# The input projection of a hybrid trunk as seven block products for eight

## The chip, the cores and the metric

One core of a Trainium2 chip (trn2). The metric is the device time of one execution in microseconds (us); lower is better.

## The reference

One layer over x (2,048 tokens by 1,024 channels, float32). The input projection takes RMS-normed x through one weight of 1,024 by 10,256 columns; its columns feed a state space mixer, a windowed attention, a short convolution, and three merge gates.

```python
h = rms_norm(x, norm_pre)
proj = h @ w_in
(z, xbc, dt_raw, q, k, v, g_attn, u, b_sc, c_sc, g_sc, merge) = split(proj)
y_ssm = ssd_branch(z, xbc, dt_raw, ...)              # xbc: silu(conv4(xbc) + b); z: silu
y_attn = attention_branch(q, k, v) * silu(g_attn)
y_sc = b_sc * conv3(c_sc * u) * silu(g_sc)
merged = sum(sigmoid(merge_i) * (y_i @ p_i))
out = x + rms_norm(merged @ w_out, norm_post)
```

## The kernel before

Five stages run one after another: the input projection (`projection_stage`, L88 to L596), the SSD scan with the second half of the gates (`ssd_gates_stage`), attention, the merging of the branches, the output. The change is in the first; the second only reads its operands in another layout.

Every float32 product is made of three matmuls on values split in a high part (rounded to `float32r`) and a low part (the rest): hi x hi, hi x lo, lo x hi. In the projection the weight tile (128 channels of the contraction by 128 columns) is the stationary operand, and 512 tokens of h move.

The opening (L299 to L310 on PE): x comes in 16 tiles of 128 tokens; DVE sums the squares (L486), ACT takes the root (L353) and scales (L359), POOL multiplies by `norm_pre` (L258), PE turns the tile (L279), ACT takes the high part (L363) and DVE the low one (L496). The turned h stays in two buffers, `h0` for the first half of the tokens and `h1` for the second. The dt product is interleaved with it.

Then 88 tiles of 128 columns follow in the loops from L311 on. `product` (L291) waits for its weights and its accumulator and makes 96 matmuls, 24 for each of four spans of 512 tokens; the 24 gate tiles make the first half of the tokens alone, 48 matmuls. Two slots alternate, each with four banks of PSUM, so a slot's tile is read while the other is made. The order is that of the columns: z, xbc, q, k and v, g, sc, gates.

```python
for c in chunks:
    h_hi, h_lo = (h[t // 2][:, t % 2 * 4:t % 2 * 4 + 4, part, c] for part in range(2))
    pe.matmul(to, w_hi[:, slot, c], h_hi, start=c == 0, stop=False)
    pe.matmul(to, w_hi[:, slot, c], h_lo, start=False, stop=False)
    last = pe.matmul(to, w_lo[:, slot, c], h_hi, start=False, stop=c == KC - 1)
```

SP loads each weight tile (512 KB, L166) once its slot's weights are made. POOL rounds it (L247) and subtracts (L249) when the slot's product has ended. ACT evacuates z, k, v, g and the gates (L393) and issues their stores; xbc is convolved by DVE out of PSUM (L523, L528), then ACT's silu; q is split by ACT (L423) and DVE (L540); sc is multiplied by DVE (L549 to L561). The chain that makes dt and its sums (L566 to L595) runs among the gates.

Of the kernel before, what the change touches and what calls it, by code (L numbers as in the profile page):

```python
# [10 lines left out]

# [5 lines left out]
F32 = mybir.dt.float32  # L17
# [4 lines left out]
P = 128  # L22
# [65 lines left out]
def projection_stage(nc, w, d, h, wt, v, ident, eps):  # L88
# [9 lines left out]
    pairs = {"z": SSM // P // 2, "xbc": (C_DT - C_XBC) // P // 2, "q0": KV // P // 2, "q1": KV // P // 2,  # L98
             "q2": KV // P // 2, "kv": 2 * KV // P // 2, "g": KV // P // 2,
             "sc": 4 * SC // P // 2, "gates": 3 * DM // P // 2}  # L100
    base, n_pairs = {}, 0
    for kind, n in pairs.items():
        base[kind] = n_pairs
        n_pairs += n
    with ExitStack() as stack:
        s = Scope(nc, stack)
        cleared, cleared_sems = s.cleared_sem, lambda name, n: [s.cleared_sem(f"{name}{i}") for i in range(n)]
        raw, w_hi, w_lo, work = wt["raw"], wt["w_hi"], wt["w_lo"], wt["work"]
        stage = s.sb("p_stage", [P, 2, SEQ])
# [4 lines left out]
        w_pre = s.sb("n_wpre", [P, DM])  # L114
        ssum, std, rstd = (s.sb(n, [P, 4]) for n in ("n_ssum", "n_std", "n_rstd"))
        acc = s.ps("p_acc", [P, 2, SEQ])

        x_sb = stage[:].rearrange("p a (b n) -> p (a b) n", n=DM)
        x_scaled, h_tok = (work[:, k].rearrange("p (b n) -> p b n", n=DM) for k in range(2))
        tr = acc[:, 1].rearrange("p (b n) -> p b n", n=DM)  # L120
        squared = raw[:, 1].rearrange("p c n -> p (c n)")

        dt_raw = work[:HEADS, 0]
        t0, t1, t2, t3 = (work[:, 1, j * TILES * HEADS:(j + 1) * TILES * HEADS] for j in range(4))
        ps_dt, ps_cs, ps_last = (acc[:, 1, at:at + TILES * HEADS] for at in (2 * BANK, 3 * BANK, 3 * BANK + TILES * HEADS))
# [1803 lines left out]
```

## Time and profile before

| | |
|---|---|
| time, median of 3 runs (lowest to highest) | 3249.74 us (3247.03 to 3251.0) |
| the profiled execution's own time | 3249.21 us |
| its span, first to last instruction | 3247.6 us |
| busy PE, PE weight load | 3074.1 us (95%), 2586.7 us (80%) |
| busy DVE, ACT, POOL | 1071.6, 861.0, 752.0 us (33, 27, 23%) |
| granted TensorE clock, mean | 0.979 |
| DMA, mean over the span | 119 GB/s |

The profile is of one execution. "Busy" of PE is counted from the start to the modelled end of each matmul, which overlap: a matmul of 512 columns is shown with about 0.39 us while the next starts 0.23 us after it. The pitch from start to start is what a matmul costs. A line such as L286 is a line of the kernel's source; PEld is the loading of stationary weights.

### The profile page before, as it was taken

The page shows a single profiled execution, that of the slowest core. Times are in us where ns is not written, and L with a number is a line of the kernel's source. Part 1 is how long each engine was busy: PE and PEld are TensorE (multiplying, and loading weights), DVE is VectorE, ACT ScalarE, POOL GpSimd, SP SyncE. Part 2 cuts the span into 40 slices and gives each one's busy share as a digit, 9 for nine tenths or more (in the row PEclk, how much of TensorE's full clock was granted, in tenths as well). Part 3 has the DMA queues.
Part 4 walks back from the last instruction along what each step waited for, and adds up shares of the span by engine and source line. Part 5 has one row for each costly group of instructions (what it writes and reads, how often), then busy time and mean ns, then how long its engine had stood idle before and what let it go on. Part 6 is the DMA issues. An engine that isn't in the chain of part 4 may idle for free. (4 is left out here: it accounts for less than half of the span.)

```text
span 3247.6 us, 41561 instructions
## 1 busy us (share of the span) xinstructions
PE 3074.1 (95%) x15182; PEld 2586.7 (80%) x15182; DVE 1071.6 (33%) x1824; ACT 861.0 (27%) x1461; POOL 752.0 (23%) x390
## 2 busy tenths in 40 slices
PE   6999999999999999999998999998999968989898
PEld 5888888888888888888887778777898856778687
DVE  6003444201000011110001544444565567762333
ACT  5110000000000000000112555554566542332232
POOL 7111111111111111112322443442111034321000
PEclk9999999999999999999999999998999989999999
DMA  5121121344412201112234564564534457775543
GB/s 156 58 77 65 71 77 68 93 117 129 116 59 77 77 20 38 39 39 86 97 97 132 148 174 136 155 174 171 157 119 144 144 176 237 235 244 145 174 136 116
DMA packets 335884, 387.70 MB, mean 119 GB/s; under 512 B 23104, under 2 KB 284480, under 8 KB 320192
## 3 DMA queue, kind: packets, MB, share of 16 engines
q1 hardware_dynamic: 317440, 287.42, 30.0%
q10 hardware_dynamic: 16080, 91.23, 8.1%
q0 software_dynamic: 2304, 8.39, 0.7%
q8 instruction: 21, 0.34, 0.0%
q14 instruction: 39, 0.32, 0.0%
HBM read 251.21 MB, written 135.79 MB: 119 GB/s over the span
## 5 line engine op out<-in xcount | busy, mean ns | idle before, releaser
L286 PE MATMUL p_acc<-h,w_hi 128*128 128x512 f32 x2464 | 970.0, 394 | 3.8 <-DVE h L496 3.5
L288 PE MATMUL p_acc<-h,w_lo 128*128 128x512 f32 x2464 | 966.0, 392 | 0.0
L287 PE MATMUL p_acc<-h,w_hi 128*128 128x512 f32 x2464 | 960.2, 390 | 0.0
L288 PEld LDWEIGHTS p_acc<-h,w_lo 128*128 128x128 f32 x2464 | 463.1, 188 | 103.9
L286 PEld LDWEIGHTS p_acc<-h,w_hi 128*128 128x128 f32 x2464 | 463.7, 188 | 100.5 <-DVE h L496 4.8
L287 PEld LDWEIGHTS p_acc<-h,w_hi 128*128 128x128 f32 x2464 | 463.3, 188 | 101.0
L247 POOL CAST w_hi<-raw 128x1024 fp32r<-128x1024 f32 x88 | 91.4, 1039 | 1350.9 <-PE p_acc L288 1344.9
L1598 PE MATMUL b_acc<-b_yhi,b_whi 128*128 128x512 f32 x512 | 205.7, 402 | 43.8 <-DVE b_ylo_ssd L1689 25.8
L249 POOL TENSOR_TENSOR w_lo<-raw,w_hi 128x1024 fp32r<-128x1024 f32 x88 | 212.1, 2410 | 7.1
L393 ACT ACTIVATE p_stage<-p_acc 128x1024 f32<-128x1024 f32 (+1 forms) x45 | 64.2, 1427 | 554.3 <-PE p_acc L288 554.2
L1600 PE MATMUL b_acc<-b_yhi,b_wlo 128*128 128x512 f32 x512 | 202.6, 396 | 0.0
L1245 ACT ACTIVATE a_probs<-a_scores,a_att 128x256 f32<-128x256 f32 (+1 forms) x384 | 155.7, 454 | 108.4 <-DVE a_att L1278 106.9
L1278 DVE CUSTOM_DVE_ANT_0 a_scores<-a_pss,a_band 128x256 f32<-128x256 f32 (+1 forms) x384 | 125.1, 364 | 142.7 <-PE a_pss L1183 116.7
L779 PE MATMUL s_acc<-h,w_hi 128*128 128x512 f32 x384 | 168.5, 439 | 0.0
L523 DVE TENSOR_SCALAR work<-p_acc,p_cw,p_cb 128x2048 f32<-128x2048 f32 x16 | 38.6, 2411 | 384.4 <-PE p_acc L288 384.4
L1215 PE MATMUL a_pso<-a_vt,a_probst 128*128 128x65 f32 x1200 | 156.2, 269 | 1.5 <-DVE a_att L1291 1.5
L1598 PEld LDWEIGHTS b_acc<-b_yhi,b_whi 128*128 128x128 f32 x512 | 98.4, 192 | 69.8 <-issue 36.5
L781 PE MATMUL s_acc<-h,w_lo 128*128 128x512 f32 x384 | 152.5, 397 | 0.0
L780 PE MATMUL s_acc<-h,w_hi 128*128 128x512 f32 x384 | 152.5, 397 | 0.0
L1215 PEld LDWEIGHTS a_pso<-a_vt,a_probst 128*128 128x128 f32 x1200 | 149.9, 193 | 2.0 <-DVE a_att L1291 1.8
L549 DVE TENSOR_TENSOR work<-p_acc,work 128x2048 f32<-128x2048 f32 x4 | 9.2, 2292 | 417.4 <-PE p_acc L288 417.4
L1183 PE MATMUL a_pss<-a_khi,a_q 128*128 128x256 f32 (+1 forms) x384 | 128.1, 356 | 19.6 <-DVE a_att L1278 19.1
(195 smaller groups left out, 4141.4 us busy)
## 6 DMA issues: line engine op xcount, KB each, us to landing
raw<-w_in SPq DMA_DIRECT2D x113, 512.0 KB, 4.4
a_q<-s_qs SPq DMA_DIRECT2D x27, 1024.0 KB, 4.9
b_gate<-s_gates SPq DMA_DIRECT2D x48, 512.0 KB, 7.1
s_xbc<-p_stage ACTq DMA_DIRECT2D x16, 1024.0 KB, 3.9
work<-s_xbc SPq DMA_DIRECT2D x16, 1024.0 KB, 7.1
s_sums<-s_cs SPq DMA_DIRECT2D x16, 1024.0 KB, 5.1
b_att<-s_att SPq DMA_DIRECT2D x24, 528.0 KB, 5.6
s_qs<-p_stage ACTq DMA_DIRECT2D x24, 512.0 KB, 5.5
```

The lines of the kernel that those rows point to most:

```text
L249: pool.tensor_tensor(w_lo[:, slot], raw[:, slot], w_hi[:, slot], ALU.subtract).then_inc(w_made[slot], 1)
L286: pe.matmul(to, w_hi[:, slot, c], h_hi, start=c == 0, stop=False)
L287: pe.matmul(to, w_hi[:, slot, c], h_lo, start=False, stop=False)
L288: last = pe.matmul(to, w_lo[:, slot, c], h_hi, start=False, stop=c == KC - 1)
L779: pe.matmul(acc_tiled, w_hi[:, slot, b], hi, start=b == 0, stop=False)
L780: pe.matmul(acc_tiled, w_hi[:, slot, b], lo, start=False, stop=False)
L781: last = pe.matmul(acc_tiled, w_lo[:, slot, b], hi, start=False, stop=b == KC - 1)
L1183: last = pe.matmul(bank[:, (e + 1) * 2 * P - n:(e + 1) * 2 * P], q_s[:, g, at:at + P], keys, start=first, stop=not first)
L1215: last = pe.matmul(ps_o[:, j // 2 % 2, (b + e) % 4, :OUT_W], probs_t[:, j % 4, 2 * e + h], v_tok[:, g, b + e - 1 + h, sl * OUT_W:(sl + 1) ...
L1245: last = act.activation(probs[:, j % 4, e, 2 * P - n:], scores[:, j % 4, e, 2 * P - n:], ACT.Exp, bias=att[:, g, b + e, 2 * OUT_W + sl:2 * ...
L1598: pe.matmul(to, w_hi[:, k, c], y_hi[:, c, span], start=c == at, stop=False)
L1600: last = pe.matmul(to, w_lo[:, k, c], y_hi[:, c, span], start=False, stop=c == at + n - 1)
```

## The change

The projection's weights of two tiles (256 columns) and 1,024 tokens are seen as 2 by 2 blocks on each side: A11, A12 are the two halves of the contraction of the first tile, A21, A22 those of the second; B11, B21 are the two halves of the contraction for 512 tokens, B12, B22 for the next 512. Instead of 8 block products of 12 matmuls, 7 are made (Winograd's form of Strassen's scheme), each of 12 matmuls over 4 chunks. A "set" is the seven products of one pair of tiles for one half of the tokens: 44 sets for the first half (gates, kv, g, q, xbc, sc, z) and 32 for the second, 76 in all, unrolled.

- Weight sums, POOL: four passes of 128x512 a set (`add_sums`), then seven subtractions for the low parts (`lo`). The high parts go to ACT (`split_weight`), each after the product of the set before that read the same buffer. `w_hi` and `w_lo` hold seven blocks, once.
- Products, PE: X, R0, R1, W, X, R0, W name the banks of the seven; four banks of PSUM serve them, each once. The other four are for the convolution.
- Output sums: ACT copies product 1 (`product_one`), DVE makes seven sums of 128x512 a set, into the stage or, for q, xbc and sc, into a padded buffer in SBUF, from which the convolution now reads; two small buffers carry the last tokens of the first half to the second.
- Activations: B11, B22 and so on and T1 to T4, their differences, are made once for each half, split into seven operands of 128x2048, which take the place of `h0` and `h1`. For the second half the blocks are prepared during sets 1 to 12 through DRAM (`s_h`, `s_t`), and the seven operands are loaded and split again at the turn, sets 43 and 44.
- dt is two products of 32 columns, 32 matmuls each, after sets 41 and 44, and its chain runs in sets 46 to 48. All stores are issued by SP, none by ACT.

The diff, cut to its core (setup of buffers, the order's tables, the dt chain and the preparation of B are left out):

```diff
-                def span_of(slot, t, chunks=range(KC)):
...
-                with pe.Fori(0, base["gates"]) as i:
-                    product(1, i)
-                    product(0, i + 1)
...
+                for u in range(NSETS):
+                    half = SETS[u][2]
+                    for k in range(PRODUCTS):
+                        bank = acc[:, bank_of[k]]
+                        if u in (0, TURN):
+                            pe.wait_ge(op_ready[k], half + 1)
+                        pe.wait_ge(w_made, PRODUCTS * u + k + 1)
+                        if k == 0 and u:
+                            pe.wait_ge(mixed_in, SUMS * u - 2)
+                        if k == 1 and u:
+                            pe.wait_ge(mixed_in, SUMS * u - 1)
+                        if k == 3 and u:
+                            pe.wait_ge(mixed_in, SUMS * u)
+                        if k == 4:
+                            pe.wait_ge(p1_made, u + 1)
+                        if k == 5:
+                            pe.wait_ge(mixed_in, SUMS * u + 1)
+                        if k == 6:
+                            pe.wait_ge(mixed_in, SUMS * u + 4)
+                        for c in range(4):
+                            hi, lo = (x[:, k, c * P:(c + 1) * P] for x in (w_hi, w_lo))
+                            pe.matmul(bank, hi, ops[k][:, 0, c], start=c == 0, stop=False)
+                            pe.matmul(bank, hi, ops[k][:, 1, c], start=False, stop=False)
+                            last = pe.matmul(bank, lo, ops[k][:, 0, c], start=False, stop=c == 3)
+                        last.then_inc(prod, 1)
...
-                def split(slot, use, n):
-                    pool.wait_ge(raw_loaded[slot], 16 * use + 16)
-                    wait_alone(pool, acc_made[slot], use + 1, carried)
-                    pool.tensor_copy(w_hi[:, slot], raw[:, slot]).then_inc(hi_ready, 1)
-                    pool.wait_ge(hi_ready, n + 1)
-                    pool.tensor_tensor(w_lo[:, slot], raw[:, slot], w_hi[:, slot], ALU.subtract
-                                       ).then_inc(w_made[slot], 1)
...
+                def lo(u, k):
+                    if u:
+                        pool.wait_ge(hi_made, PRODUCTS * (u - 1) + k + 1)
+                    tt(w_lo[:, k], weight(u, k), w_hi[:, k], ALU.subtract).then_inc(w_made, 1)
+
+                def add_sums(u):
+                    a11, a12, a21, a22 = (raw[u % 2 * 2 + m][:, 4 * k:4 * k + 4].rearrange("p c n -> p (c n)")
+                                          for m in range(2) for k in range(2))
+                    tt(sums[:, 0], a21, a22, ALU.add).then_inc(sums_made, 1)
+                    pool.wait_ge(sums_made, 4 * u + 1)
+                    tt(sums[:, 1], sums[:, 0], a11, ALU.subtract).then_inc(sums_made, 1)
+                    tt(sums[:, 2], a21, a11, ALU.subtract).then_inc(sums_made, 1)
+                    pool.wait_ge(sums_made, 4 * u + 2)
+                    tt(sums[:, 3], a12, sums[:, 1], ALU.subtract).then_inc(sums_made, 1)
...
+                def product_one(u):
+                    act.wait_ge(prod, PRODUCTS * u + 1)
+                    if u:
+                        act.wait_ge(mixed_in, SUMS * u - 2)
+                    act.activation(p1 if u else p1_first, acc[:, X], ACT.Copy).then_inc(p1_made, 1)
+
+                def split_weight(u, k):
+                    act.wait_ge(prod, PRODUCTS * (u - 1) + k + 1)
...
+                    act.activation(w_hi[:, k], weight(u, k), ACT.Copy).then_inc(hi_made, 1)
...
+                    if u:
+                        finish(u - 1)
...
+                    tt(t_now, acc[:, R0], p1 if u else p1_first, ALU.add).then_inc(mixed_in, 1)
...
+                    tt(u_now, acc[:, R1], t_now, ALU.add).then_inc(mixed_in, 1)
...
+                    tt(out_block(u, 1, 1), acc[:, W], u_now, ALU.add).then_inc(mixed_in, 1)
+                    tt(t_now, acc[:, W], t_now, ALU.add).then_inc(mixed_in, 1)
...
+                    tt(out_block(u, 0, 0), acc[:, X], p1 if u else p1_first, ALU.add).then_inc(mixed_in, 1)
+                    dve.wait_ge(prod, PRODUCTS * u + 6)
+                    tt(out_block(u, 0, 1), acc[:, R0], u_now, ALU.add).then_inc(mixed_in, 1)
...
+                    tt(out_block(u, 1, 0), acc[:, W], t_now, ALU.add).then_inc(mixed_in, 1)
```

How the order moves, at three places. On POOL, before, one pass of the loop over two weight tiles (`raw` are the loaded tiles):

```order
L247 CAST w_hi<-raw 128x1024 [waits p_acc_made1]
L248 ISA
L249 TENSOR_TENSOR w_lo<-raw,w_hi 128x1024 [waits p_hi_ready]
L245 ISA
L84 REGISTER_ALU [waits p_raw_loaded0]
L247 CAST w_hi<-raw 128x1024 [waits p_acc_made0]
```

and now, one set (`p_sums` are the four weight sums, `p_hi_r` ACT's high parts):

```order
L398 TENSOR_TENSOR p_sums<-raw 128x512 [waits p_hi_r,p_w_made,p_raw_loaded1,p_raw_loaded0]
L400 TENSOR_TENSOR p_sums<-p_sums,raw 128x512 [waits p_sums_r]
L401 TENSOR_TENSOR p_sums<-raw 128x512
L403 TENSOR_TENSOR p_sums<-raw,p_sums 128x512 [waits p_sums_r]
L393 TENSOR_TENSOR w_lo<-raw,w_hi 128x512 [waits p_hi_r]
L393 TENSOR_TENSOR w_lo<-p_sums,w_hi 128x512 [waits p_hi_r] x3
L393 TENSOR_TENSOR w_lo<-raw,w_hi 128x512 [waits p_hi_r]
```

With the two that follow, eleven passes of 512 stand where two casts and two subtractions of 1,024 stood for as many columns, and they are made once for each half of the tokens.

On DVE, before, the convolution of one xbc tile:

```order
L523 TENSOR_SCALAR work<-p_acc,p_cw,p_cb 128x2048
L527 ISA
L528 ISA [waits p_conv_step]
L528 SCALAR_TENSOR_TENSOR work<-p_acc,p_cw,work 128x2045
L527 REGISTER_ALU
L528 ISA [waits p_conv_step]
L528 SCALAR_TENSOR_TENSOR work<-p_acc,p_cw,work 128x2046
```

and now, from the sixth sum of a set to the first sums of the next (`p_halo` carries tokens between the halves, `p_sums_r2` counts the sums, `p_prod` the products):

```order
L875 TENSOR_TENSOR work<-p_acc,work 128x512 [waits p_prod]
L709 COPY work<-p_halo 128x3 [waits p_posted]
L713 COPY p_halo<-work 128x3 [waits p_sums_r2,p_step]
L714 TENSOR_SCALAR p_acc<-work,p_cw,p_cb 128x1024
L718 SCALAR_TENSOR_TENSOR p_acc<-work,p_cw,p_acc 128x1024 [waits p_step]
L887 TENSOR_TENSOR work<-p_acc,work 128x512 [waits p_sums_r2,p_prod]
L718 SCALAR_TENSOR_TENSOR p_acc<-work,p_cw,p_acc 128x1024 [waits p_step] x2
L709 COPY work<-p_halo 128x3 [waits p_posted]
L713 COPY p_halo<-work 128x3 [waits p_sums_r2,p_step]
L714 TENSOR_SCALAR p_acc<-work,p_cw,p_cb 128x1024
L718 SCALAR_TENSOR_TENSOR p_acc<-work,p_cw,p_acc 128x1024 [waits p_step] x3
L811 TENSOR_TENSOR work<-p_acc,work 128x512 [waits p_sums_r2,p_p1_r,p_prod]
```

The sums that release PSUM banks now stand between the passes of the convolution.

On PE, the step from one product to the next, before (once in 96 or 48 matmuls) and now (once in 12):

```order
L293 REGISTER_ALU [waits p_w_made1]
L286 MATMUL p_acc<-h0,w_hi 128x512 [waits p_acc_taken1]
L287 MATMUL p_acc<-h0,w_hi 128x512
L288 MATMUL p_acc<-h0,w_lo 128x512
```

```order
L489 MATMUL p_acc<-h_kept,w_lo 128x512
L487 MATMUL p_acc<-p_ops,w_hi 128x512 [waits p_sums_r2,p_w_made]
L488 MATMUL p_acc<-p_ops,w_hi 128x512
```

`h_kept` and `p_ops` hold the operands of the seven products. 6,384 matmuls of L487 to L489 and 64 of the dt products stand where 7,392 of L286 to L288 were executed.

## Rows read from the trace of the kernel before

**Rows 1.** The page's busy time by engine.
```profile
PE 3074.1 (95%) x15182; PEld 2586.7 (80%) x15182; DVE 1071.6 (33%) x1824; ACT 861.0 (27%) x1461; POOL 752.0 (23%) x390
```

**Rows 2.** Groups by line (busy, mean ns, idle before, releaser), and L288's own answer.
```profile
L286 PE MATMUL p_acc<-h,w_hi 128*128 128x512 f32 x2464 | 970.0, 394 | 3.8 <-DVE h L496 3.5
L247 POOL CAST w_hi<-raw 128x1024 fp32r<-128x1024 f32 x88 | 91.4, 1039 | 1350.9 <-PE p_acc L288 1344.9
L249 POOL TENSOR_TENSOR w_lo<-raw,w_hi 128x1024 fp32r<-128x1024 f32 x88 | 212.1, 2410 | 7.1
...
L288 PE MATMUL p_acc<-h,w_lo x2464: 388/392/629, 30.6 to 1741.4; 128*128 128x512 f32 x190
```

**Rows 3.** Stretches of time: length, busy us of PE, PEld, DVE, ACT, POOL, PEclk, DMA share, GB/s.
```profile
1000.00:1200.00 200.00, 200.00 (x877) 164.44 (x876) 11.47 (x5) 13.21 (x7) 31.02 (x18) 1.00 0.18 56
1740.00:1750.00 10.00, 4.05 (x19) 3.38 (x18) 1.23 (x1) 3.61 (x4) 1.03 (x2) 0.84 0.36 115
```

**Rows 4.** PE in order of time, projection (start us, us).
```profile
71.74 0.50 PE L286 MATMUL p_acc<-h,w_hi 128*128 128x512 f32 x1 [0.26 <-POOL w_lo L249]
72.08 0.39 PE L287 MATMUL p_acc<-h,w_hi 128*128 128x512 f32 x1
...
1339.62 0.39 PE L288 MATMUL p_acc<-h,w_lo 128*128 128x512 f32 x1
...
1343.92 0.40 PE L286 MATMUL p_acc<-h,w_hi 128*128 128x512 f32 x1
```

**Rows 5.** PE in order of time, output stage; 13 matmuls stand between the two.
```profile
3149.65 0.39 PE L1833 MATMUL o_acc<-o_wlo,o_mhi 128*128 128x512 f32 x1
...
3152.82 0.39 PE L1832 MATMUL o_acc<-o_whi,o_mhi 128*128 128x512 f32 x1
```

**Rows 6.** Lines of POOL (ns, min/median/max) and of DVE (groups), several stages.
```profile
L1474 POOL TENSOR_TENSOR b_wlo<-b_raw,b_whi x20: 1266/4616/4959, 2638.4 to 3005.2; 128x2048 fp32r<-128x2048 f32 x12, 128x1536 fp32r<-128x1536 f32 x4, 128x512 fp32r<-128x512 f32 x4
...
L1486 POOL TENSOR_TENSOR b_att<-b_att x8: 1619/1630/2147, 2665.9 to 2851.5; 128x512 f32<-128x512 f32 x8
...
L258 POOL TENSOR_TENSOR work<-work,n_wpre x16: 2338/3314/3410, 9.4 to 59.7; 128x1024 f32<-128x1024 f32 x16
...
L909 DVE TENSOR_TENSOR s_cbm<-s_psm,v_tri 128x512 f32<-128x512 f32 x16 | 11.1, 692 | 76.7 <-PE s_psm L805 69.4 <-DMA s_norm<-ssm_norm 7.3
...
L1689 DVE TENSOR_TENSOR b_ylo<-b_ylo,b_yhi 128x1024 fp32r<-128x1024 f32 x12 | 20.3, 1750 | 6.1 <-ACT b_yhi L1508 6.1
```

**Rows 7.** POOL, then DVE, each in order of time, around two sc tiles.
```profile
1366.19 1.04 POOL L247 CAST w_hi<-raw 128x1024 fp32r<-128x1024 f32 x1 [18.40 <-PE p_acc L288]
1367.31 2.41 POOL L249 TENSOR_TENSOR w_lo<-raw,w_hi 128x1024 fp32r<-128x1024 f32 x1
...
1389.24 2.41 POOL L249 TENSOR_TENSOR w_lo<-raw,w_hi 128x1024 fp32r<-128x1024 f32 x1
...
1366.13 2.29 DVE L558 TENSOR_TENSOR work<-p_acc,work 128x2048 f32<-128x2048 f32 x1 [12.28 <-PE p_acc L288]
...
1390.00 3.80 DVE L561 TENSOR_TENSOR p_stage<-p_stage,work 128x2048 f32<-128x2048 f32 x1 [21.58 <-ACT p_stage L448]
```

**Rows 8.** Groups by line and shape, projection.
```profile
L528 DVE SCALAR_TENSOR_TENSOR work<-p_acc,p_cw,work 128x2047 f32<-128x2047 f32 x16 | 37.6, 2350 | 2.4 <-DVE work L528 2.3
...
L393 ACT ACTIVATE p_stage<-p_acc 128x1024 f32<-128x1024 f32 x24 | 24.6, 1025 | 231.4 <-PE p_acc L288 231.4
```

**Rows 9.** All engines in order of time, the opening.
```profile
6.27 1.23 DVE L486 CUSTOM_DVE_ANT_0 raw<-p_stage 128x1024 f32<-128x1024 f32 x1 [0.22 <-DMA p_stage<-x]
...
11.80 1.94 PE L279 MATMUL p_acc<-ident,work 128*128 128x128 f32 x8 [11.80 <-POOL work L258]
...
35.06 1.03 PE L279 MATMUL p_acc<-ident,work 128*128 128x128 f32 x8
```

**Rows 10.** DMA issues: KB each, median us from issue to landing.
```profile
a_q<-s_qs SPq DMA_DIRECT2D x27, 1024.0 KB, 4.9
...
work<-s_xbc SPq DMA_DIRECT2D x16, 1024.0 KB, 7.1
```

More of the change, by code:

```diff
@@ new lines, in weight, with wait_stage, out_block @@
+        def weight(u, k):
+            which = weight_of[k]
+            if which[0] == "s":
+                return sums[:, which[1]]
+            return raw[u % 2 * 2 + which[1]][:, which[2] * 4:which[2] * 4 + 4].rearrange("p c n -> p (c n)")
+        def wait_stage(eng, u, slot):
+            n = stores_before(u, slot)
+            if n:
+                eng.wait_ge(stored[slot], 16 * n)
+        def out_block(u, m, n):
+            at = slice(n * BANK, (n + 1) * BANK)
+            return body[m][:, at] if padded(SETS[u][0]) else stage[:, u % 2 * 2 + m, at]
@@ new lines, in _ @@
+                        last = pe.transpose(acc[:, c, j * P:(j + 1) * P], x_tile(j)[:, c * P:(c + 1) * P], ident[:])
+                last.then_inc(turned, 1)
+                pe.wait_ge(scaled, 8)
+                for c in range(KC):
+                    pe.wait_ge(ev_dve if c % 2 else ev_act, c // 2 + 1)
+                    for j in range(4):
+                        last = pe.transpose(acc[:, c, j * P:(j + 1) * P], x_tile(4 + j)[:, c * P:(c + 1) * P], ident[:])
+                last.then_inc(turned, 1)
@@ new lines, in _, with dt_product @@
+                pe.wait_ge(ev_act, 8)
+                pe.wait_ge(ev_dve, 8)
+                def dt_product(half):
+                    pe.wait_ge(dtw_made, 4)
+                    for n, terms in enumerate((((0, 0), (4, 4)), ((8, 5), (0, 3)))):
+                        for first, k in terms:
+                            for c in range(4):
+                                for part in range(2):
+                                    last = pe.matmul(acc[:2 * HEADS, CV + n], dt_w[:, first + c], ops[k][:, part, c],
+                                                     start=(first, k, c, part) == (*terms[0], 0, 0),
+                                                     stop=(first, k, c, part) == (*terms[1], 3, 1))
+                    last.then_inc(dt_prod, 1)
@@ L771, in gates @@
                             j, part = 3 * k + half // 2, half % 2
-                            slot, first = (j // 2 + 2) % 3, 4 * (j % 2)
+                            slot = (j // 2 + 2) % 3
                             if part == 0:
```

1058 lines of the change are left out of this document (626 added, 432 removed).

## Prediction

> **What bounds the kernel now.** I read the page's table of busy time first: PE is busy for 95% of the span, every other engine for a third or less [rows 1]. The groups by line then show where: the input projection's three matmuls (L286 to L288), 2,464 each, 7,392 in all [rows 2]. The stretches of time show them alone on the path: PE is busy for 200.00 of 200 us at a granted clock of 1.00 and falls to 4.05 of 10 where the stage ends [rows 3]. Inside it the others wait for PE, not the reverse: POOL's L247 sat idle 1,344.9 us before L288 released it [rows 2]. So a matmul less is its whole pitch saved, as long as the others keep up with the rest. After the opening the 7,296 matmuls from 71.74 us (the first of the weight tile after the dt product [rows 4]) to 1741.4 [rows 2] take 1,669.7 / 7,295 = 0.2289 us each; the end of a product runs at 0.2263 (19 steps from 1339.62 to 1343.92 [rows 4]), and the output stage, with a whole 512-wide operand and a wait every six matmuls, at 3.17 / 14 = 0.2264 [rows 5].
>
> **What goes and what comes on PE.** 7,392 matmuls go. 76 sets of 7 products of 12 matmuls come, 6,384, and 64 for dt: 944 fewer, each still 512 wide. For the pitch of the new ones the two bounds are 0.2264 [rows 5] and 0.2289; I take 0.2278, between them, since the order of waits is like the output stage's but a product alternates between operand buffers. A set is then 84 x 0.2278 = 19.1 us, a product 2.73 us.
>
> **POOL's share of a set.** 11 passes of 128x512, where the tile before had a cast and a subtraction of 128x1024. A subtraction takes 2,410 ns for 1,024 [rows 2] and at best 1,266 for 512 [rows 6]; with the 0.08 us between the cast (1366.19 + 1.04) and its follower (1367.31) [rows 7] that is 11 x 1.35 = 14.8 of 19.1 us. The set's last w_lo waits for the last product of the set before, but its reader is six products (16 us) away; the next four sums and six subtractions fit in between. I cost it at nothing; the cover is 4.3 us a set, and once it is gone every microsecond is one on PE, 75 times.
>
> **DVE's share.** Seven passes of 512 with one operand in PSUM, 0.69 each (L909 [rows 6]): 4.8 us. In the 16 xbc sets come two tiles of one scaled copy and three taps at 1,024: by halves of the 2,350 for 2,047 [rows 8], about 1.2 each, 9.8 us, and about 2 us of halo copies and hand-overs: 16.6 of 19.1. By position: the last sum ends 1.6 us into the next set (R0's sum, the copy and one or two taps of the first tile lie ahead of it), the remaining taps reach to about 10 us, T's sum is made at 10.7 and product 5 asks for it at 13.6. It fits with 3 us to spare, at nothing. Shorter kinds have more room. **ACT** has seven halves of a 1,025 ns copy [rows 8], P1's copy and two 1,024-wide passes: about 0.59 x 8 + 2.1 = 6.8 us, hidden.
>
> Here a contention shows: L561, both operands in SBUF, took 3.80 us from 1390.00, while POOL subtracted from 1389.24 to 1391.65; L558, 2,048 as well but with one operand in PSUM, took 2.29 from 1366.13, beside POOL's cast and 1.1 us of its subtraction [rows 7]. POOL's 2,410 did not grow. The sums of this change read PSUM, so I take them as L558; the q tiles' subtraction, the gated products of sc and the operand splits do not.
> The Trainium skill (SBUF — State Buffer, section "Who interferes with whom") says that a DVE instruction with two SBUF inputs and a GpSimd one that reads SBUF exclude each other for a whole instruction, so POOL would also be held: by that rule a q set gives POOL 14.8 + 2.4 us, still under 19.1, and the sum stays within its range. The trace agrees on DVE's side (1391.65 + 2.29 = 1393.94 against 1393.80 measured); POOL being held shows in L258's 3,314 ns against 2,338 at best [rows 6].
>
> **The opening.** Before, the first product starts near 30 and the first weight tile after dt at 71.74 [rows 2, 4]. Now nothing of set 0 can start before all eight x tiles of the first half are scaled and turned. The second tile is read at 6.27 [rows 9]; with two weight loads between, at 1.5 to 2 us for each 512 KB, the eighth lands near 22. ACT's square and root and DVE's scale put it at 27; 32 transposes at the cold pace (1.94 for 8) end near 34, the evacuations near 37. Then product 0 starts, and the next operands follow one another: the differences T1 to T4 on DVE (2.3 each, up to 3.8 beside POOL), each split by ACT (1.9) and DVE (2.3). Passing down that chain: T1 39, T2 42, operand 1 ready 46, operand 2 49, operand 3 55, operand 6 62, the sums after it 64, and product 6 ends about 67; with the slow first matmuls set 1 starts at **69**. From both sides: 60 with every pass at its lone time, 85 if each of the nine DVE passes waits for POOL (9 x 1.5 more).
>
> **What else is put on PE.** B's transposes: eight groups of eight, 1.03 each warm [rows 9], 8.2 us. Those of dt and cs and two small matmuls, as before, about 3. The dt products 64 x 0.2278 = 14.6. **At the turn** between the halves seven operands of 1 MB are loaded as the products release them (4.9 us from issue to landing [rows 10]) and split by ACT (1.9) and DVE (seven passes of 2.3, or 3.8 beside POOL) among the running sums: DVE has 16 to 27 us more work within two sets and 13 us of room. By position operand 0 is ready at 16 of 19, operands 3 to 6 each a microsecond or two late: 6 us, between 0 and 20. The dt chain (L783 to L805) holds PE about 1 us. The B preparation through DRAM in sets 0 to 12 waits on SP for loads and stores of 1 MB or less (4.9 and 7.1 us [rows 10]) with a set of 19.1 us per step: at nothing; behind those waits on SP stand the weight loads, issued a set ahead, and the stores, whose slot is asked for 9 us into the second next set.
>
> **Sum.** End of the last product: 69 + 75 x 84 x 0.2278 (1,435.1) + 14.6 + 8.2 + 3 + 6 + 1 = 1,536.9, against 1,741.6 now: -204.7. The tail (POOL's last subtraction, silu of two tiles, a store) is 1.5 us longer than the 7 to 9 us now. The next stages keep their work. -203 from the profiled execution's 3,249.21 is **3,046 us**; that execution stands 0.5 below the median of the runs, which changes nothing.
>
> **Rivals.** (1) *Each product pays a hand-over.* 532 products start with a wait; where PE did wait, the first matmul's step was 0.34 instead of 0.23 (71.74 to 72.08 [rows 4]). 532 x 0.11 = +58: 3,104. For it: four banks, each read by DVE before reuse. Against: by position all are free 2 us or more ahead, and [rows 5] shows none. (2) *DVE is late in the xbc sets*: at the 1,750 ns that the dearest 1,024-wide pass takes (L1689 [rows 6]), eight passes are +4.2, 20.8 in all, 1.7 x 16 = +27: 3,073. (3) *POOL paces mildly*: at L1486's 1,695 ns [rows 6] the eleven are 19.5 us with gaps: 0.4 x 75 = +30: 3,076. (4) *POOL paces and the kernel is slower*: the saving is 203 / 75 = 2.7 us a set, gone once a set lasts 21.8 us, i.e. a POOL pass of 1.91 us. L1486's dearest is 2.147: 11 x 2.23 = 24.5, +405: 3,451. For it: POOL shares with DVE, and DVE is now busy in every set. Against: [rows 7] shows POOL at its pace, 2.41, beside L561. (5) *The change does not remove work*: excluded by the order of instructions for PE, unless the opening or the turn gives it back, which their upper bounds (16 and 14) don't.
> Unrolled code is a lesser one: PE has 7,742 rows for 2,059. The Trainium skill (Runtime: NRT & Kernel Launch, section "Instruction fetch mechanics") says straight code is fetched ahead and mostly hidden, taken branches not; no row here has so long a straight piece, so it neither adds nor takes.
>
> **How the numbers follow.** The forecast 0.71, (1) 0.08, (2) 0.07, (3) 0.07, (4) 0.03, other delays below the saving 0.04. The low end takes the pitch of 0.2264 (-9), the opening at 60 (-9) and no loss at the turn (-6): 3,022. The high end adds to the forecast the opening's 16, the turn's 14 and the pitch's 8, and takes in (2) and (3): 3,085. That leaves out (1), (4) and some of the rest, 0.15 to 0.2. A measurement of this kernel tells 0.2% (6.5 us) from no change: faster 0.96, same 0.01, slower 0.03.
>
> **What would show it.** Right: 6,384 matmuls at a pitch near 0.228 and PE at 100% from about 70 us on; the stage's last product ending near 1,537; POOL's 512-wide subtraction at 1.2 to 1.3 us; gaps on PE only before 70 us and around the middle. Wrong: PE idle in every set with POOL's w_lo as releaser (3, 4), in xbc sets with DVE (2), or a step of 0.34 at each product's first matmul (1).

## The result and the profile after

| | before | after |
|---|---|---|
| median | 3250.37 us | 3060.57 us (3056.77 to 3064.43) |
| ratio | | 0.9419, 95% interval 0.9398 to 0.9441 |
| profiled execution | 3249.21 us | 3064.23 us (span 3062.6) |
| last matmul of the projection starts at | 1741.4 us | 1553.4 us |

One of the four executions of the kernel before took 4392.04 us and is left out of the ratio; without it the median is 3249.74.

The kernel is 5.8% faster. The forecast was 3,046, the range 3,022 to 3,085: the time lies inside the range and 14.6 us above the forecast.

The page of after, busy time by engine, which answers to [rows 1]:

```profile
PE 2874.0 (94%) x14238; PEld 2412.6 (79%) x14238; DVE 1587.1 (52%) x2540; ACT 1211.7 (40%) x2094; POOL 1569.2 (51%) x1044
```

PE has 944 records less (15,182 to 14,238), exactly the difference that the prediction counts, and is busy 200 us less; POOL has doubled (752 to 1,569), DVE went from 1,072 to 1,587. The share of PE in the span is the same as before, 94 against 95%: the kernel is bound as it was, by less work.

The page's groups of after, and the answer for line L489, which answer to [rows 2] (busy us, mean ns | idle before, releaser; then ns min/median/max, first and last start):

```profile
L487 PE MATMUL p_acc<-h_kept,w_hi 128*128 128x512 f32 x1216 | 482.2, 397 | 14.3 <-DVE h_kept L673 7.8
L393 POOL TENSOR_TENSOR w_lo<-p_sums,w_hi 128x512 fp32r<-128x512 f32 x304 | 406.6, 1354 | 153.5 <-ACT w_hi L571 153.2
...
L571 ACT ACTIVATE w_hi<-p_sums 128x512 fp32r<-128x512 f32 x300 | 189.5, 632 | 492.1 <-PE p_acc L489 472.2
...
L489 PE MATMUL p_acc<-h_kept,w_lo x1216: 388/389/632, 34.1 to 1550.6; 128*128 128x512 f32 x174
L489 PE MATMUL p_acc<-p_ops,w_lo x912: 388/392/628, 43.7 to 1553.4; 128*128 128x512 f32 x183
```

Read the idle column: ACT's copies sat idle 472.2 us until PE's L489 released them, and POOL's subtraction waited for ACT 153.2 us. The order of who waits for whom is PE, then ACT, then POOL (before, POOL made the high parts itself and waited for PE directly); the weight chain is behind PE in time, not ahead of it. This pass of POOL is 1,354 ns on average, where the prediction took 1.35 with its gap.

Stretches of time of after, which answer to [rows 3] (length, busy us of PE, PEld, DVE, ACT, POOL, PEclk, DMA share, GB/s):

```profile
0.00:40.00 40.00, 17.98 (x76) 15.88 (x76) 22.15 (x27) 23.36 (x37) 27.15 (x26) 0.79 0.50 157
40.00:70.00 30.00, 19.54 (x67) 15.46 (x68) 23.77 (x12) 11.68 (x12) 28.46 (x16) 0.77 0.19 53
540.00:690.00 150.00, 150.00 (x656) 122.81 (x655) 141.44 (x147) 51.87 (x78) 110.67 (x87) 1.00 0.35 109
1300.00:1500.00 200.00, 200.00 (x875) 163.74 (x874) 90.69 (x100) 55.34 (x88) 152.77 (x115) 1.00 0.27 77
1550.00:1560.00 10.00, 3.76 (x17) 2.75 (x15) 3.68 (x3) 4.75 (x4) 2.41 (x1) 0.91 0.27 105
```

In steady sets PE is at 200.00 of 200 at a granted clock of 1.00. The convolutions of the xbc sets (540 to 690) are the densest stretch for DVE, 141.44 of 150, and PE loses nothing there. POOL is at 152.77 of 200 from 1,300 on, or 14.7 us a set against 14.8 predicted. The opening (40 to 70) is different: PE 19.54 of 30, POOL 28.46 of 30. The last row holds the stage's end, where PE falls to 3.76 of 10.

All of PE's waits of after from 40 to 1,560 us (us in total, times, longest):

```profile
PE p_acc L487 <- DVE h_kept L673: 7.8, 1, 7.8
PE p_acc L510 <- DVE v_all L801: 4.5, 1, 4.5
PE p_acc L487 <- DVE p_ops L673: 4.2, 1, 4.2
PE p_acc L487 <- DVE p_stage L873: 3.7, 1, 3.7
PE p_acc L487 <- DVE work L832: 0.4, 1, 0.4
```

Five waits, 20.6 us, all of them with DVE as releaser and none in a steady set: two in set 0 (7.8, 4.2), one at the turn (3.7), one in the dt chain (4.5), and 0.4 in set 3, beside the preparation of B. None has POOL's `w_lo`.

The same terms as in the prediction's sum, by the starts of the sets in the trace of after:

| term | predicted | measured | difference |
|---|---|---|---|
| set 1 starts | 69 | 71.3 | +2.3 |
| 75 sets of 84 matmuls | 1,435.1 (19.13 each) | 1,444.0 (19.25 each) | +8.9 |
| dt products (behind sets 41 and 44) | 14.6 | 14.8 | +0.2 |
| transposes of B (sets 1 to 8, with the wait of 0.4) | 8.2 | 7.8 | -0.4 |
| transposes of dt and cs (the 3 predicted held the two small matmuls too) | 3 | 1.7 | -1.3 |
| the turn (sets 43, 44) | 6 | 5.8 | -0.2 |
| dt chain with the two small matmuls (set 47: 27.38 instead of 19.25) | 1 | 8.1 | +7.1 |
| end of the last product | 1,536.9 | 1,553.6 | +16.7 |
| the rest of the span, longer than before by | 1.5 | 3 | +1.5 |

That is the profiled execution, 18 us above the forecast; its run lies 3.7 above the median. Three terms carry the miss: the pitch, the dt chain and the opening. The experiments below go at these, and before that at the ground under the forecast: that PE's work sets the time.

### The profile page after: what moved, and what is told of

It reads as the page before. It is cut to its first block and busy times, and to the rows that moved or that the text cites. A ratio compares the mean times of both kernels' runs of the same rounds, so it can differ in the third digit from the quotient of the medians.

```text
span 3062.6 us, 41517 instructions
## 1 busy us (share of the span) xinstructions
PE 2874.0 (94%) x14238; PEld 2412.6 (79%) x14238; DVE 1587.1 (52%) x2540; ACT 1211.7 (40%) x2094; POOL 1569.2 (51%) x1044
## 5 line engine op out<-in xcount | busy, mean ns | idle before, releaser
L487 PE MATMUL p_acc<-h_kept,w_hi 128*128 128x512 f32 x1216 | 482.2, 397 | 14.3 <-DVE h_kept L673 7.8
L393 POOL TENSOR_TENSOR w_lo<-p_sums,w_hi 128x512 fp32r<-128x512 f32 x304 | 406.6, 1354 | 153.5 <-ACT w_hi L571 153.2
L489 PE MATMUL p_acc<-h_kept,w_lo 128*128 128x512 f32 x1216 | 478.7, 394 | 0.0
L488 PE MATMUL p_acc<-h_kept,w_hi 128*128 128x512 f32 x1216 | 476.6, 392 | 0.0
L571 ACT ACTIVATE w_hi<-p_sums 128x512 fp32r<-128x512 f32 x300 | 189.5, 632 | 492.1 <-PE p_acc L489 472.2
L487 PE MATMUL p_acc<-p_ops,w_hi 128*128 128x512 f32 x912 | 360.9, 396 | 4.6 <-DVE p_ops L673 4.2
L489 PE MATMUL p_acc<-p_ops,w_lo 128*128 128x512 f32 x912 | 358.3, 393 | 0.0
L488 PE MATMUL p_acc<-p_ops,w_hi 128*128 128x512 f32 x912 | 355.9, 390 | 0.0
L487 PEld LDWEIGHTS p_acc<-h_kept,w_hi 128*128 128x128 f32 x1216 | 230.2, 189 | 63.7 <-DVE h_kept L673 8.2
L489 PEld LDWEIGHTS p_acc<-h_kept,w_lo 128*128 128x128 f32 x1216 | 230.2, 189 | 52.3
L488 PEld LDWEIGHTS p_acc<-h_kept,w_hi 128*128 128x128 f32 x1216 | 230.4, 189 | 50.5
L487 PEld LDWEIGHTS p_acc<-p_ops,w_hi 128*128 128x128 f32 x912 | 171.8, 188 | 42.1 <-DVE p_ops L673 4.9
L489 PEld LDWEIGHTS p_acc<-p_ops,w_lo 128*128 128x128 f32 x912 | 171.5, 188 | 40.8
L488 PEld LDWEIGHTS p_acc<-p_ops,w_hi 128*128 128x128 f32 x912 | 171.6, 188 | 38.2
```

The lines of the kernel that those rows point to most:

```text
L393: tt(w_lo[:, k], weight(u, k), w_hi[:, k], ALU.subtract).then_inc(w_made, 1)
L487: pe.matmul(bank, hi, ops[k][:, 0, c], start=c == 0, stop=False)
L488: pe.matmul(bank, hi, ops[k][:, 1, c], start=False, stop=False)
L489: last = pe.matmul(bank, lo, ops[k][:, 0, c], start=False, stop=c == 3)
L571: act.activation(w_hi[:, k], weight(u, k), ACT.Copy).then_inc(hi_made, 1)
```

## The experiments

The kernel before ran beside every one of them; its medians were 3245.53 to 3249.65 us. Later stages vary by some 15 us from one execution to the next (the rest after the projection was 1,502 to 1,523 us in these traces, at unchanged code), so for a change inside the projection the start of its last matmul in the trace is the sharper measure. All but e1 to e3 keep the amount of work. e1, e2, e3, e5, e6 and e10 have two executions each. Products are counted from 0 here, as in the code; the expectations count them from 1.

**e1: an eighth product.** Product 4 is made twice a set, on PE alone.

```diff
-                        for c in range(4):
+                        for c in list(range(4)) * (2 if k == 4 else 1):
```

> Product 5 of every set is made twice, 12 matmuls more in each of 76 sets, so eight products a set as without the block scheme; the result stays the same. Theory (PE's count of matmuls is the whole price): 912 x 0.227 = +207 us, 3,268 us, and about 18 us over the kernel before, which is what the opening, the turn and the dt chain cost. Rival (the others set the pace of a set, so PE has room): well under +150 us.

Measured: 3273.71 us, ratio 1.0079 (1.0053 to 1.0105). A set lasts 21.97 us, 2.72 more than after's 19.25; the last matmul starts at 1754.0, 200.7 later than in after. The gain comes wholly from the product left out: with eight products and all the rest of the change in place the kernel is 0.8% slower than before.

**e2 and e3: more work on POOL.** From set 2 on the first weight sum is made two or five times more, each waited for.

```diff
+                    for j in range(5 if u > 1 else 0):      # e2: range(2 ...)
+                        tt(sums[:, 0], a21, a22, ALU.add).then_inc(padded_made, 1)
+                        pool.wait_ge(padded_made, 5 * (u - 2) + j + 1)
                     tt(sums[:, 0], a21, a22, ALU.add).then_inc(sums_made, 1)
```

> POOL makes the first weight sum three times from set 2 on, two passes of 1.3 us more a set. Theory (POOL has some 4 us a set to spare): no change, within 5 us of 3,061. Rival (POOL sets the pace already in part): +2.7 x 74 = up to +200 us.

> Five passes more a set: 15.1 + 6.8 = 21.9 us of POOL in a set that lasts 19.25. Theory: POOL becomes the bound, 2.6 x 74 = +195 us, 3,255 us, as slow as the kernel before, with PE waiting for w_lo in every set. Rival (POOL's work is not what PE would wait for): no change.

Measured: e2 3085.29 us, ratio 0.9499 (0.9468 to 0.9530); e3 3217.91, ratio 0.9907 (0.9888 to 0.9927). The stretch of steady sets in e2, and then in e3:

```profile
1300.00:1500.00 200.00, 200.00 (x875) 163.75 (x874) 99.86 (x108) 55.62 (x90) 180.19 (x136) 1.00 0.28 81
```

```profile
1300.00:1500.00 200.00, 189.01 (x801) 149.97 (x799) 153.90 (x146) 55.33 (x91) 195.37 (x152) 0.99 0.30 92
```

With two passes more POOL is busy 180.19 of 200 us and PE still 200.00, with the same 875 matmuls: that cover exists. With five POOL is at 195.37 and PE at 189.01. (By then e3 is behind, so its stretch holds xbc sets and DVE's figures are not comparable.) PE's two most frequent waits of e3 from 70 to 1,712 us name first the releaser that rivals 3 and 4 spoke of:

```profile
PE p_acc L491 <- POOL w_lo L394: 76.2, 45, 3.8
PE p_acc L491 <- DVE work L815: 15.4, 17, 1.1
```

Of the 17 waits for L815, 14 stand in sets 25 to 32 and 56 to 61, in the xbc sets or just behind them: with POOL this full, DVE comes last there, as rival 2 has it. The sets of e3 that wait last 20.8 to 23.8 us and the projection ends 159 us later. In e2 the steady sets are unchanged, but set 3 (26.6 us), set 26 (20.4) and set 44 (36.0) are longer than in after, and the projection ends 15.3 us later. So its cost is not in the equal sets: set 3 stands beside the preparation of B, set 44 is the turn, and only 1.2 us lie in an xbc set (26). The stages behind the projection took 12.7 us more in the same execution; that part is not put down to the edit.

**e4 to e6: where the operands lie.** What is sought here is why a set lasts 19.25 us and not the 19.04 of 84 steps at 0.2267. In after, products 0, 3, 4 and 5 read `h_kept`, products 1, 2 and 6 read `p_ops`. In the steady sets the products last 2.77, 2.76, 2.75, 2.77, 2.72, 2.72 and 2.76 us. Below are the seams of products 0, 1, 2 and 3 in the PE timeline of after (start us, us):

```profile
1300.31 0.39 PE L489 MATMUL p_acc<-h_kept,w_lo 128*128 128x512 f32 x1
1300.54 0.40 PE L487 MATMUL p_acc<-p_ops,w_hi 128*128 128x512 f32 x1
1300.78 0.40 PE L488 MATMUL p_acc<-p_ops,w_hi 128*128 128x512 f32 x1
...
1303.30 0.40 PE L487 MATMUL p_acc<-h_kept,w_hi 128*128 128x512 f32 x1
1303.54 0.39 PE L488 MATMUL p_acc<-h_kept,w_hi 128*128 128x512 f32 x1
```

The step at a product's first matmul (1300.31 to 1300.54) is 0.23, not 0.34, and the 12 steps of the product from 1300.54 to 1303.30 take 2.76. A hand-over would be one long step at the seam; here the excess is spread over the matmuls. Products 4 and 5, which begin with the same kind of wait but follow a product on `h_kept`, run at 2.72 / 12 = 0.2267. This pointed at the place of the moving operand in SBUF.

The change from one buffer to the other has a price too, though not at the seam. Products 0 and 3 read `h_kept` like 4 and 5, but right behind a product on `p_ops`, and take 2.77 instead of 2.72; by the medians of the steady sets their first ten steps lie between 0.224 and 0.236 us and the last two are at 0.227. Product 2, behind another on `p_ops`, repeats 0.232, 0.226 and 0.229, 2.75 in all. So of the 0.21 us that a set lasts too long, 0.08 is the pace on `p_ops` (three products) and 0.13 comes with the four changes (0.05 twice, 0.016 twice).

e4 puts `h_kept` behind the weights and the vectors, e5 `w_hi` and `w_lo` ahead of everything, e6 `raw` and `work` ahead of it:

```diff
-            kept = k.sb("h_kept", [P, 4, 2, 4, BANK], F32R)
             wt = {"raw": ..., "w_hi": ..., "w_lo": ..., "work": ...}
...
+            kept = k.sb("h_kept", [P, 4, 2, 4, BANK], F32R)
```

> The operands h_kept are allocated after the weights and above them instead of below, p_ops stays where it is. Theory (the pitch of 0.229 against 0.227 us goes with the place of the moving operand in SBUF, high ones being slower): all seven products at 2.76 us, a set at 19.3, +5 us. Rival (it goes with the hand-over to another product or with the weights' place): products 1, 4, 5 and 6 stay as they are, or all become 2.72 because the weights have moved, 75 x 0.21 = -16 us.

> Order of allocation: the split weights first, then h_kept (about 29 to 93 KB of each partition), then the rest; p_ops unchanged. Theory A (a moving operand is slow above some address near 64 KB): products 1 and 5 (B11, B21, below 61 KB) at 2.72 us, 4 and 6 (B12, B22) slower. Theory B (it is slow when it lies above the weights it meets): all seven products at 2.75, a set at 19.23 us, as with h_kept high. Either way within 10 us of 3,061.

> The split weights are allocated after h_kept (about 25 to 89 KB) and above it, at 89 to 117 KB. Theory A: the products of B12 and B22 (4 and 6) slow, near 2.75 in the middle of a product. Theory B: as in the changed kernel, products 5 and 6 at 2.72, a set at 19.25 us.

Measured: e4 3062.95 us, ratio 0.9425 (0.9409 to 0.9442), last matmul at 1552.5, and all seven products at 2.75, so that products 4 and 5 have lost their 2.72. The answer for the last matmul's line in e4 has 392 ns on `h_kept`, where after has 389:

```profile
L489 PE MATMUL p_acc<-h_kept,w_lo x1216: 388/392/628, 34.1 to 1549.8; 128*128 128x512 f32 x174
```

The 5 us that were expected on top did not come: products 0 and 3 went from 2.77 to 2.75, a set lasts 19.23, and where both buffers run at the same pace a change between them costs nothing. e5 3066.82, ratio 0.9453 (0.9429 to 0.9477), and e6 3070.74, ratio 0.9465 (0.9439 to 0.9491): both leave each product as in after, and the projection ends at 1551.9 and 1552.2, so their higher medians don't come from the products. Moving the moving operand itself alone mattered; moving the weights did not. Neither theory on the order of the two holds.

**e9 and e10: a shift of `p_ops` by 64 and by 32 bytes**, with an unused tile allocated ahead of it:

```diff
+            k.sb("v_pad", [P, 16])                     # e10: [P, 8]
             projection_stage(nc, w, d, kept, wt, v, v_all, ident, eps)
```

> A tensor of 64 bytes a partition, never used, is allocated ahead of p_ops, so that p_ops starts at 143,136 instead of 143,072 in each partition, the same remainder by 128 (32 instead of 96) as h_kept. Theory C (the pitch of 0.229 us goes with the remainder of the moving operand's address): all seven products at 2.72 us, a set at 19.04 instead of 19.25, 75 x 0.21 = -16 us: 3,045 us. Rival (it goes with the tensor or with some other neighbour): a set stays at 19.25 us.

> The same with 32 bytes: p_ops has the remainder 0, h_kept and the weights keep 32. If only a remainder of 96 is slow, as e9: a set at 19.04 us. If the operand must have the weights' remainder: 19.25 us.

Measured: e9 3062.62 us, ratio 0.9433 (0.9412 to 0.9454), products 2.73, 2.79, 2.80, 2.73, 2.72, 2.72, 2.79, set 19.29, last matmul at 1556.7. e10 3073.22, ratio 0.9459 (0.9434 to 0.9484), products 2.76, 2.81, 2.80, 2.76, 2.72, 2.72, 2.82, set 19.39, last at 1562.3. The answers for the last matmul's line (ns min/median/max) in e9 and e10:

```profile
L489 PE MATMUL p_acc<-h_kept,w_lo x1216: 387/389/628, 33.5 to 1553.9; 128*128 128x512 f32 x174
L489 PE MATMUL p_acc<-p_ops,w_lo x912: 390/397/632, 43.8 to 1556.7; 128*128 128x512 f32 x183
```

```profile
L489 PE MATMUL p_acc<-h_kept,w_lo x1216: 387/389/628, 32.9 to 1559.5; 128*128 128x512 f32 x174
L489 PE MATMUL p_acc<-p_ops,w_lo x912: 392/399/632, 43.7 to 1562.3; 128*128 128x512 f32 x183
```

The median on `p_ops` goes from 392 to 397 and 399 ns, while `h_kept`, which did not move, stays at 389. So the place of the moving operand does set the pitch (the products on `p_ops` are 1 to 2% longer by a shift of 64 or 32 bytes), and the price of a change moves with it (products 0 and 3, whose own operand stayed, go from 2.77 to 2.73 and 2.76). But the rule that I had made of it (the remainder of the address by 128, Theory C) is refuted: with the same remainder as `h_kept` all seven were to take 2.72, and the products on `p_ops` became slower.

**e7: the dt chain's two matmuls two products later.**

```diff
-                        if k == 2 and u == CHAIN + 1:
+                        if k == 4 and u == CHAIN + 1:
```

> PE's two small products for the sums of dt (set 47) stand after product 5 instead of product 3. Theory (the 8.1 us that set 47 lasts too long are PE waiting for DVE's dt chain, then a half clock): DVE's chain is done 13 us into the set, product 5 ends at 13.7, so -7 to -8 us: 3,053 us. Rival (PE would stop anyway, at product 6, for the sum of T that DVE makes after the chain): less than 2 us gained.

The DVE timeline of after around the chain (start us, us):

```profile
990.55 1.34 DVE L789 TENSOR_SCALAR v_all<-work 128x256 f32<-128x256 f32 x1
991.92 1.41 DVE L791 TENSOR_TENSOR work<-work,v_all 128x256 f32<-128x256 f32 x1
993.25 1.52 DVE L792 TENSOR_TENSOR work<-work,v_all 128x256 f32<-128x256 f32 x1
994.81 1.75 DVE L794 RECIPROCAL work<-work 128x256 f32<-128x256 f32 x1
...
999.36 0.42 DVE L801 SCALAR_TENSOR_TENSOR v_all<-v_all,p_alog 128x256 f32<-128x256 f32 x1
```

The answer for L583 of the kernel before, a pass of the same chain and shape (one of several that read 0.42 or 0.43), and three rows of its timeline at that place:

```profile
L583 DVE TENSOR_TENSOR work<-work x1: 428/428/428, 1574.8 to 1574.8; 128x256 f32<-128x256 f32 x1
...
1564.89 2.40 POOL L249 TENSOR_TENSOR w_lo<-raw,w_hi 128x1024 fp32r<-128x1024 f32 x1
...
1565.18 2.38 DVE L569 SCALAR_TENSOR_TENSOR work<-work 128x256 f32<-128x256 f32 x1
...
1572.76 1.75 DVE L580 RECIPROCAL work<-work 128x256 f32<-128x256 f32 x1
```

In before the chain stood among the gates, and POOL was idle for most of it (from 1567.3 to 1576.05). Here it stands beside POOL's 1.3 us passes, and passes that took 0.29 (L573, L575), 0.36 or 0.43 us take 1.0 to 1.5: a chain of dependent small passes pays half to nearly a whole POOL pass for each. The 1.75 of RECIPROCAL is its own length, the same in both kernels. The kernel before had the warning in it: the one pass of its chain that met a POOL pass, L569, took 2.38 us and ended 0.3 behind it. What that does on PE, in the PE timeline of after:

```profile
994.95 0.40 PE L489 MATMUL p_acc<-p_ops,w_lo 128*128 128x512 f32 x1
999.84 1.22 PE L510 MATMUL p_acc<-v_all,v_tri 128*128 128x256 f32 x2 [4.49 <-DVE v_all L801]
1000.85 1.06 PE L511 MATMUL p_acc<-v_all,v_ones 128*128 128x256 f32 x2
1001.35 0.99 PE L487 MATMUL p_acc<-h_kept,w_hi 128*128 128x512 f32 x1
```

PE waits 4.49 us and comes back at the lower clock: 1.22 us for the two matmuls of L510, then eight matmuls at a step of 0.43 us in place of 0.23 (the first of them comes late). The granted clock of that stretch of after is 0.50 (columns as above):

```profile
1000.50:1004.50 4.00, 4.00 (x11) 3.15 (x10) 0.68 (x1) 0.00 (x0) 0.00 (x0) 0.50 0.00 0
```

In e7's PE timeline the same line comes without a wait:

```profile
1000.19 0.39 PE L489 MATMUL p_acc<-h_kept,w_lo 128*128 128x512 f32 x1
1000.71 0.70 PE L510 MATMUL p_acc<-v_all,v_tri 128*128 128x256 f32 x2
1001.24 0.59 PE L511 MATMUL p_acc<-v_all,v_ones 128*128 128x256 f32 x2
1001.49 0.58 PE L487 MATMUL p_acc<-h_kept,w_hi 128*128 128x512 f32 x1
```

Measured: 3058.34 us, ratio 0.9431 (0.9416 to 0.9447). Set 47 takes 20.56 us instead of 27.38, and the last matmul starts at 1546.3, 7.1 earlier, 6.8 of it from set 47. That set repeats well: 20.5 to 20.6 us in the three traces with this edit, 27.3 to 27.7 in those of after, e4 to e6 and e8 to e10. DVE's chain is as slow as in after (the same passes read 1.35, 1.41 and 1.52); PE only no longer stands behind it. On the median's interval alone this can't be told from after; on the trace it can.

**e8: the order of DVE's and POOL's passes in the opening.** POOL waits with its two large subtractions (`lo_of_block`) until DVE has made the sum and the operand that PE asks for first:

```diff
                     if u == 0:
+                        pool.wait_ge(t_made, 3)
                         lo_of_block(4, b_raw[B21])
+                        pool.wait_ge(op_ready[3], 1)
                         lo_of_block(5, b_raw[B22])
```

> POOL's two 4.6 us passes on operands 5 and 6 wait until DVE has made the third difference, and the second of them until operand 4 is ready. Theory (PE's longest gap in the opening, 7.8 us before product 4, is DVE held out by POOL's pass): DVE's 6.7 us pass falls to 2.3, product 4 starts 4 to 5 us earlier, and 2 to 4 us are kept at set 1. Rival (the chain of ACT and DVE after it takes it back): no change.

In the opening of after, the DVE timeline and then the POOL timeline:

```profile
42.56 3.68 DVE L673 TENSOR_TENSOR p_ops<-p_stage,p_ops 128x2048 fp32r<-128x2048 f32 x1
46.16 6.69 DVE L694 TENSOR_TENSOR work<-work 128x2048 f32<-128x2048 f32 x1
...
54.83 2.90 DVE L673 TENSOR_TENSOR h_kept<-work,h_kept 128x2048 fp32r<-128x2048 f32 x1 [1.98 <-ACT h_kept L539]
```

```profile
39.48 4.61 POOL L407 TENSOR_TENSOR h_kept<-p_stage,h_kept 128x2048 fp32r<-128x2048 f32 x1
44.03 6.67 POOL L407 TENSOR_TENSOR h_kept<-work,h_kept 128x2048 fp32r<-128x2048 f32 x1
```

And in e8, where L694 is L696:

```profile
45.29 2.28 DVE L696 TENSOR_TENSOR work<-work 128x2048 f32<-128x2048 f32 x1
```

```profile
47.66 4.65 POOL L407 TENSOR_TENSOR h_kept<-p_stage,h_kept 128x2048 fp32r<-128x2048 f32 x1 [10.87 <-DVE work L696]
```

Measured: 3058.35 us, ratio 0.9428 (0.9412 to 0.9444). Alone, DVE's pass takes 2.28 us and POOL's 4.65. In after the passes take turns, and a pass is shown from its issue, with the time that it is held: POOL's first ends at 44.09 and DVE's split 2.15 later (46.24), POOL's second 4.46 after that (50.70), DVE's L694 2.15 after that (52.85). So 6.69 and 6.67 are each a wait for the other's pass and a pass of its own. The order decides which one PE waits for: set 1 starts at 68.1 instead of 71.3, the last matmul at 1549.9, 3.5 earlier. Set 1 starts at 66.9 to 68.8 in the three traces with this edit and at 70.2 to 71.5 in the others of the same work. The longest of PE's waits falls from 7.8 to 5.7 us.

**e11 and e12: what helped, together.** e11 has e7's, e8's and e9's edits, e12 has e7's and e8's.

> The three edits together: dt's two products after product 5 of set 47, POOL's two passes of the opening later, 64 bytes ahead of p_ops. If the three lie on the path one after another: -6.8 - 3.2 - 16 = -26 us, 3,035 us, with the projection's last product ending near 1,528 instead of 1,553.6.

> The two edits that shortened the projection, without the 64 bytes: dt's two products after product 5 of set 47, POOL's two passes of the opening later. If they add up: the last product starts 6.8 + 3.2 = 10 us before 1553.4, near 1,543.4, sets stay at 19.25 us, and the time is about 3,051 us. If the one is taken back by the other: 1,546 to 1,550.

Measured: e11 3057.57 us, ratio 0.9405 (0.9387 to 0.9423), set 19.29 us, last matmul at 1548.7; e12 3055.11, ratio 0.9398 (0.9371 to 0.9425), set 1 at 66.9, set 47 at 20.54 us. The last matmul's line in e12 (L491 there):

```profile
L491 PE MATMUL p_acc<-p_ops,w_lo x912: 392/392/628, 43.1 to 1541.9; 128*128 128x512 f32 x183
```

It starts last at 1541.9, 11.5 us before after's 1553.4 and within 2 of what was expected; e7's 7.1 and e8's 3.5 add up to 10.6. e11 missed what was expected of it because the padding costs time instead of saving it. e12 has the lowest median of all the kernels, 5.5 us under after; the two intervals overlap, so for the whole kernel a difference to after is not shown, while the shorter projection is.

## Why the prediction came out as it did

**What bounds the kernel: right.** "A matmul less is its whole pitch saved" is what e1 tested from the other side: 912 matmuls put back cost 200.7 us within the projection and the whole gain. In after PE waits in no steady set.

**What is hidden: right, with one gap in it.** POOL was given 14.8 us of a set and took 14.7 (15.1 between 300 and 500 us, read from that stretch), DVE was given 16.6 in the xbc sets and was busy 141.44 / 150 x 19.25 = 18.2, so of the 2.5 us that I had left it only 1.1 was there; it was enough. e2 shows a cover of two more POOL passes at 200.00 of 200 on PE; e3 shows where it ends. The break-even in rival 4, 21.8 us a set, is about where e3 lies: its sets that wait last 20.8 to 23.8 us, and 0.9% is left of a gain of 5.8. The gap: the cover of 4.3 us holds for a steady set. I expected nothing for e2 and it took 15, in the few sets that do something besides.

**The rivals.** (1), at 0.11 us for each product, falls by two readings: the step at the seam is 0.23 us, and products 4 and 5 wait as the others and run at 0.2267. A change of buffer does cost something, 0.13 us a set or about 10 us in all, spread over the matmuls behind it. (2) and (3) fall by the waits: none in an xbc set, none for `w_lo`. (4) did not occur, and e3 shows it is a real mechanism at five passes more. (5) fell at the count of 944. The 1,695 ns that (3) takes from [rows 6] is the mean of L1486's eight passes; the row gives their median, 1,630.

**The first step that failed: "The dt chain (L783 to L805) holds PE about 1 us."** It is the term of the sum that was furthest off for its size: set 47 was 8.1 us too long, 6.8 of it the chain's, for the two small matmuls themselves take 1.3 (20.56 against 19.25 in e7). The rule for it was in the prediction already, for two large passes (3.80 for 2.29 beside POOL [rows 7]); I did not carry it to this chain. The short ones pay most for their length, because each of them may have to wait out a POOL pass of 1.3 us. And the wait itself, 4.5 us, is two thirds of the price: the rest, a little over 2 us, is the half-speed clock after it. e7 takes away both with DVE's chain unchanged, and set 47 gives back 6.8.

**The second: the pitch of 0.2278, chosen between 0.2264 and 0.2289.** It measured 19.25 / 84 = 0.2292, just above the upper bound, and 8.9 us in all. I chose the value in the middle because a product has one operand and the order of waits is like the output stage's. What decides is not the order of the waits but where the moving operand lies, and the change between buffers of different pace: 0.2267 where a product on `h_kept` follows another, 0.229 to 0.230 on `p_ops`, 0.231 on `h_kept` right behind `p_ops`, up to 2.82 / 12 = 0.235 on `p_ops` after a shift of 32 bytes. So "a product alternates between operand buffers" was a right reason to leave the lower bound, and too small. Why one place is slower than another stays open: e4, e9 and e10 show that the place matters, e5 and e6 that the order of the weights and `h_kept` does not, and e9 refutes the remainder by 128. The same difference was in the kernel before (0.2263 at the end of a product, 0.2289 on the mean [rows 4]); it was in the rows and I read it as noise to be averaged. Step by step its products show the same thing: the first 48 matmuls, on `h0`, run at 0.229 on the mean, the first ten on `h1` are uneven, between 0.224 and 0.236, and the rest are at 0.227.

**The third: the opening at 69.** It began 4 us sooner than predicted (33.1 against 37) and took 38.2 instead of 32. The step that failed is "2.3 each, up to 3.8 beside POOL" for DVE's passes. The bound of 3.8 came from a POOL pass of 2.41 us; beside one of 4.6 the same pass took 6.69. The Trainium skill (SBUF — State Buffer, section "Who interferes with whom") calls the ports that DVE and GpSimd share an exclusive lock, and says that a DVE instruction with two SBUF inputs contends with a GpSimd one that reads SBUF. That makes the bound the rest of POOL's pass plus the pass's own length, and not a fixed number. The trace agrees: 46.24 + 4.65 = 50.89 against POOL's end at 50.70, and 50.70 + 2.28 = 52.98 against DVE's at 52.85; e8 takes the delay away by order alone.

**The turn: right in size, not in its mechanism.** 5.8 us for 6, which is luck. I had put it on operands that come late; the trace has one wait of 3.7 us, on the bank that a sum (L873) was to free, because that sum stood on DVE behind two operand splits (2.29 from 912.70, 3.11 from 915.19). The rest, 2 us, is the lower clock after it. B's transposes, those of dt and cs and the dt products came within 1.3 us of their terms (with the 1.3 of the two small matmuls, the term of 3 is met), and the long straight piece of code on PE shows no gap in the steady stretches.

The range held because its upper part was made of the opening, the turn and the pitch; the dt chain was in none of its bounds and went through by their slack, and the pitch lay just above its own bound. Two figures of that upper part are a little too wide: nine passes of 1.5 us on 69 give 82.5 and not 85, and the pitch at 0.2289 adds 7 and not 8. With these the high end is about 3,081, and the time lies inside it all the same.

## What to carry to other kernels

Where an engine is at 100% of its time, taking work from it saves it whole as long as each of the others has cover in every step, and the steps that do something besides (opening, turn, a chain for another stage) have to be costed one by one, since the steady ones' cover does not reach them. A dependent chain of short DVE passes that read SBUF alone should be priced at up to one POOL pass each when POOL is busy, and the engine that asks for its end should ask late. A wait of 2.6 to 8 us on PE cost its length and about 2 us more here, for what followed ran at half the clock.

## What the runs showed of the chip

- *DVE and POOL take turns by whole instructions*: DVE 2.28 and POOL 4.65 us alone; where they overlap, each ends about that much after the other's end (2.15 and 4.46), so that they are shown with 6.69 and 6.67; 0.36 to 0.43 us for a 256-wide pass with both operands in SBUF alone, 1.0 to 1.5 beside POOL's passes of 1.3; 0.29 and up to 1.34 for one with a single operand (TENSOR_SCALAR, L575 before and L789 after). DVE's sums with one operand in PSUM stayed at 0.69 for 512, as taken from [rows 6].
- *A matmul's pitch depends on where its moving operand lies*: 0.2267 to 0.235 us for the same 128x512 matmul at a granted clock of 1.00, from a shift of 32 or 64 bytes or from another place in the order of allocation. Behind a change from the slower buffer to the faster one the first ten matmuls are uneven. I had not expected this; its cause is open.
- *The clock after a wait*: after PE had stood idle for 4.2, 4.5 or 7.8 us, it went on at the lower of its two levels (1.2 GHz; granted clock 0.50), with a step of 0.43 us for some 6 to 11 matmuls, then at 0.23. In e3 the waits of 1.2 to 1.9 us for POOL left the step at 0.23, and those of 2.6 to 3.8 us were followed by 6 to 14 steps of 0.43.
